# Up-projections of both layers: pairs of tiles by seven block products in place of eight

## The chip, the cores and the metric

The kernel runs on one core of one Trainium2 chip. The time is the device time of one execution in microseconds (us). Everything is float32; dense products use the float32r form of the matmul. Engines: TensorE (PE), VectorE (DVE), ScalarE (ACT), GpSimd (POOL), and SyncE (SP), which only issues DMA transfers.

## The reference, cut to what matters

Two blocks of a transformer-like model over 512 tokens plus 16 meta tokens, width 1024. The first block has two layers, and in each the part that changes is the feed-forward network:

```python
def _sq_relu_mlp(h, w1, w2):
    return jnp.square(jax.nn.relu(h @ w1)) @ w2     # w1: 1024 x 4096, w2: 4096 x 1024

for layer in range(2):
    mix = even_mixer(h, ...) if layer == 0 else retention(h, ...)
    h = layer_norm(ALPHA * h + mix, ...)
    h = layer_norm(ALPHA * h + _sq_relu_mlp(h, w1[layer], w2[layer]), ...)
```

In layer 0 all 528 columns (tokens) are computed (`wide`), in layer 1 only the 512 that the output needs.

## The kernel before, in words

Activations lie feature by feature on the 128 partitions: `x32[:, k, :]` is the k-th of 8 groups of 128 features, over T = 528 tokens. To keep float32 precision each operand is split into a high and a low part (`x_hi`, `x_lo`; `w_hi`, `w_lo`), and each product is three matmuls: w_hi x a_hi, w_hi x a_lo, w_lo x a_hi.

All weights of all stages come as one long stream of chunks, 512 KB each (8 blocks of 128 x 128). SP loads chunk g into slot g mod 4 of `raw` (L217); ACT makes `w_hi` (`split_hi`, L227), DVE makes `w_lo` (`split_lo`, L235), three chunks ahead of PE (`AHEAD`). A slot of `raw` is free when its `w_lo` is made, a slot of `w_hi` and `w_lo` when PE has finished the chunk (`chunk_done`). One chunk is one output tile of 128 features (8 input groups x 3 matmuls, and twice that many of 264 columns where the stage is wide). Four `landed` semaphores count the loads, one for each slot.

The order of each engine's work is written out by hand: each engine has its own program, in which a stage calls a split at the start of each chunk and then what belongs to the finished tile, and each runs strictly in this order. `Mlp` is the feed-forward network. The 4096 hidden features are made in two halves, a and b, of 16 tiles each: stage up (16 chunks), then stage down (16 chunks, which add into x32). For a hidden tile ACT takes the relu out of PSUM (`h_pos`), DVE squares it (`h_sq`), ACT makes `h_hi`, DVE makes `h_lo`. Tiles of a dense stage alternate between PSUM banks 0-1 and 2-3; `evicted` says when a tile is out.

Before `Mlp` stands a layer norm (`ln00`, `ln10`), behind it another (`ln01`, `ln11`). POOL adds squares for the norms, loads constants and, in the attention of layer 0, loads one row of decays for each head (`key_cum`, L492, two buffers). Before that it writes `cum_rows` to DRAM.

Of the kernel before, what the change touches and what calls it, by code (L numbers as in the profile page):

```python
# [7 lines left out]
ALU = mybir.AluOpType  # L8
ACT = mybir.ActivationFunctionType
F32 = mybir.dt.float32  # L10
# [31 lines left out]
STAGES += [("up0a", 16), ("down0a", 16), ("up0b", 16), ("down0b", 16)]  # L42
STAGES += [("ret0", 12), ("ret1", 12), ("ret2", 12), ("ret_out0", 8), ("ret3", 12), ("ret_out1", 8)]
STAGES += [("up1a", 16), ("down1a", 16), ("up1b", 16), ("down1b", 16)]
# [7 lines left out]
FIRST_CHUNK, FIRST_TILE = {}, {}  # L52
_c = _t = 0
for _n, _k in STAGES:
    FIRST_CHUNK[_n], FIRST_TILE[_n] = _c, _t
    _c += _k
    _t += 2 * _k if _n.startswith(("so", "eo")) else _k // KGROUPS.get(_n, 1)
TOTAL_CHUNKS, TOTAL_TILES = _c, _t
# [94 lines left out]
def program(nc, x_in, weights, params, tables, lam_in, w_uk, w_uv, rel, line, skewed, cum_dram, acum_dram, merged_dram, kept_dram, gate_dram, out):  # L153
    with ExitStack() as ctx:
# [55 lines left out]
        def stream_weights(sp):  # L210
            def body(g):
                s = g.mod(RING)
                if not g.stride and g.start == 1:
                    sp.wait_ge(x_landed[3], 16)
                wait(sp, lo_ready, g.at(plus=1 - RING))
                src = weights[one(g), :, :].rearrange("g p n -> p (g n)")
                sp.dma_start(raw[:, s, :, :].rearrange("p k n -> p (k n)"), src).then_inc(landed[s], 16)  # L217
            loop(sp, TOTAL_CHUNKS, RING, body, peel=1)

        def split_hi(act, g):  # L220
# [4 lines left out]
            act.wait_ge(landed[s], g.over(RING).at(16, 16))  # L225
# [247 lines left out]
        def even_loads(pool):  # L473
# [10 lines left out]
            nc.gpsimd.memset(small[:, 13:14], RMS_EPS).then_inc(forget_in, 1)  # L484
            pool.wait_ge(forget_ready, 1)
            pool.dma_start(cum_dram, neg_cum).then_inc(cum_out, 16)
            pool.wait_ge(cum_out, 16)
            for h in range(FOX_HEADS):
# [3 lines left out]
                pool.dma_start(key_cum[:, h % 2], src).then_inc(cum_in[h % 2], 16)  # L492

# [467 lines left out]
        mlp_squared, mlp_hi, mlp_lo = (sem(f"mlp_{n}") for n in ("squared", "hi", "lo"))  # L961
# [241 lines left out]
        class Mlp:  # L1203


            def __init__(self, layer, wide):
                self.layer, self.wide = layer, wide
                placed["next"] = shared
                self.h_hi = at(f"h_hi{layer}", [P, 16, T], F32R)
                self.h_lo = at(f"h_lo{layer}", [P, 16, T], F32R)  # L1210
                self.pos = at(f"h_pos{layer}", [P, 2, T])
                self.sq = at(f"h_sq{layer}", [P, 2, T])

            def pe(self, pe, norm, next_norm):
                for half, hn in enumerate("ab"):
                    pe_stage(pe, f"up{self.layer}{hn}", x_hi, x_lo, self.wide, ready=None if half else norm.ready)
                    pe_stage(pe, f"down{self.layer}{hn}", self.h_hi, self.h_lo, self.wide,
                             ready=(mlp_lo, 32 * self.layer + 16 * half), norm=next_norm if half else None)

            def act(self, act, next_norm):  # L1220
                for half, hn in enumerate("ab"):
                    name = f"up{self.layer}{hn}"

                    def keep(tile, done):
                        u = tile.plus(FIRST_TILE[name])
                        act.wait_ge(chunk_done, done)
                        wait(act, mlp_squared, tile.at(plus=32 * self.layer + 16 * half - 1))
                        nc.scalar.activation(halves(self.pos[:, tile.mod(2)], self.wide), tile_out(u, self.wide), ACT.Relu) \  # L1228
                            .then_inc(evicted[u.mod(2)], 1)
                        act.wait_ge(mlp_squared, tile.at(plus=32 * self.layer + 16 * half + 1))  # L1230
                        nc.scalar.activation(halves(self.h_hi[:, one(tile)].rearrange("p a n -> p (a n)"), self.wide),
# [1565 lines left out]
```

## Time and profile before

| | |
|---|---|
| median of 3 runs | 2895.05 us (2894.86 to 2896.65) |
| profiled execution: its own time | 2897.41 us |
| profiled execution: span of its instructions | 2895.6 us |
| PE busy | 2736.2 us (94%) |
| DVE, ACT, POOL busy | 51%, 38%, 5% of the span |
| mean granted clock of PE | 0.976 of full speed |
| DMA | 248.98 MB, mean 86 GB/s |

Busy times of different engines overlap; they say how full an engine is, not what the end waits for. The chain of waits says that: it is followed back from the last instruction to what released each step. Layer 0's network begins at about 409 us and ends at about 785 us, layer 1's runs from about 1296 to 1660 us.

### The profile page before, as it was taken

Reading aid. Unit: us, or ns where it says so; the run is one execution under the profiler, and the core shown is the slowest. Engines: PE = TensorE matmul, PEld = TensorE weight load, DVE = VectorE, ACT = ScalarE, POOL = GpSimd, SP = SyncE. Lnnn points to the kernel's source line nnn. Section 1 sums busy time; section 2 is a strip of 40 time slices with the busy share of each in tenths; the row PEclk is TensorE's granted clock in tenths of the full one; section 3 lists DMA queues with packets and bytes.
Section 4 is the critical chain, followed back from the end, with each engine's and each line's share of the span. In section 5 each row is a group of like instructions: output and inputs, shape, how many; then the busy total and the mean of one; then the engine's idle time right before and its main releaser. Section 6 shows DMA issues by size and latency. Waiting matters only on the chain.

```text
span 2895.6 us, 39470 instructions
## 1 busy us (share of the span) xinstructions
PE 2736.2 (94%) x14983; PEld 2238.0 (77%) x14983; DVE 1478.1 (51%) x2517; ACT 1095.2 (38%) x1730; POOL 151.2 (5%) x201
## 2 busy tenths in 40 slices
PE   7999989999999999979999989978999998999998
PEld 6877779999987787758888766745777776778786
DVE  3433464233433323264334434865488886664656
ACT  3455443133242322244223344345255454332322
POOL 0000020000100000010000101042000000000000
PEclk9999989999999999989999989999999999999999
DMA  4111112222221121112222224411423332222221
GB/s 154 59 45 45 45 51 94 88 88 94 81 85 63 64 94 63 59 58 95 97 92 96 86 82 117 160 41 56 140 88 117 110 110 102 80 92 97 94 92 68
DMA packets 68107, 248.98 MB, mean 86 GB/s; under 512 B 8056, under 2 KB 8056, under 8 KB 67328
## 3 DMA queue, kind: packets, MB, share of 16 engines
q1 hardware_dynamic: 58256, 210.27, 20.9%
q0 software_dynamic: 7264, 29.36, 3.6%
q10 hardware_dynamic: 2448, 7.41, 0.7%
q8 instruction: 98, 1.61, 0.2%
q14 instruction: 41, 0.34, 0.0%
HBM read 237.44 MB, written 12.71 MB: 86 GB/s over the span
## 4 chain that ended last, share of the span: by engine, by line
PE 82%; DVE 9%; ACT 5%; issue 3%; DMA 1%; POOL 0%; ACTq 0%; DVEq 0%; POOLq 0%
PE ps L264 61%; PE ps L408 6%; PE ps L1339 2%; PE ps L1618 2%; PE ps L756 2%; PE ps L635 2%; PE ps L2140 1%; DVE xs L2282 1%; DVE w_lo L235 1%; PE ps L1327 1%; ACT w_hi L227 1%; PE ps L722 1%; PE ps L1864 1%; DVE seg L2332 1%; DVE ln_xc L1166 1%
## 5 line engine op out<-in xcount | busy, mean ns | idle before, releaser
L264 PE MATMUL ps<-x_hi,w_hi 128*128 128x512 f32 (+1 forms) x2224 | 708.1, 353 | 60.8 <-DVE x_lo L1178 24.2
L235 DVE TENSOR_TENSOR w_lo<-raw,w_hi 128x1024 fp32r<-128x1024 f32 x397 | 492.4, 1241 | 419.1 <-ACT w_hi L227 409.4
L264 PE MATMUL ps<-x_lo,w_hi 128*128 128x512 f32 (+1 forms) x2224 | 703.2, 351 | 0.0
L264 PE MATMUL ps<-x_hi,w_lo 128*128 128x512 f32 (+1 forms) x2224 | 699.8, 349 | 0.0
L227 ACT ACTIVATE w_hi<-raw 128x1024 fp32r<-128x1024 f32 x397 | 416.8, 1052 | 463.3 <-PE ps L264 435.1
L264 PEld LDWEIGHTS ps<-x_hi,w_hi 128*128 128x128 f32 x2224 | 391.3, 190 | 133.2 <-issue 51.4
L264 PEld LDWEIGHTS ps<-x_lo,w_hi 128*128 128x128 f32 x2224 | 390.5, 190 | 56.1 <-issue 1.7
L264 PEld LDWEIGHTS ps<-x_hi,w_lo 128*128 128x128 f32 x2224 | 390.2, 190 | 55.5
L264 PE MATMUL ps<-h_hi,w_hi 128*128 128x264 f32 (+1 forms) x768 | 205.7, 322 | 0.0
L264 PE MATMUL ps<-h_lo,w_hi 128*128 128x264 f32 (+1 forms) x768 | 205.1, 322 | 0.0
L264 PE MATMUL ps<-h_hi,w_lo 128*128 128x264 f32 (+1 forms) x768 | 204.5, 320 | 0.0
L264 PEld LDWEIGHTS ps<-h_lo,w_hi 128*128 128x128 f32 x768 | 127.6, 188 | 11.7 <-issue 0.2
L264 PEld LDWEIGHTS ps<-h_hi,w_lo 128*128 128x128 f32 x768 | 127.8, 189 | 11.2
L264 PEld LDWEIGHTS ps<-h_hi,w_hi 128*128 128x128 f32 x768 | 127.1, 188 | 11.7 <-issue 0.2
L915 DVE SCALAR_TENSOR_TENSOR x<-x,ps 128x512 f32 (+2 forms) x56 | 38.6, 690 | 161.8 <-PE ps L264 161.8
L408 PE MATMUL ps<-x_hi,w_hi 128*128 128x264 f32 x352 | 114.0, 324 | 0.0
L1248 DVE TENSOR_TENSOR h_sq<-h_pos 128x528 f32<-128x528 f32 (+1 forms) x64 | 44.8, 700 | 127.1 <-ACT h_pos L1228 127.1
L408 PE MATMUL ps<-x_hi,w_lo 128*128 128x264 f32 x352 | 103.4, 294 | 0.0
L408 PE MATMUL ps<-x_lo,w_hi 128*128 128x264 f32 x352 | 103.4, 294 | 0.0
L1228 ACT ACTIVATE h_pos<-ps 128x528 f32<-128x528 f32 (+1 forms) x64 | 38.7, 605 | 164.7 <-PE ps L264 164.7
L408 PEld LDWEIGHTS ps<-x_hi,w_hi 128*128 128x128 f32 x352 | 69.7, 198 | 12.2 <-issue 9.9
L688 ACT ACTIVATE s_buf<-s_buf,stat 16x16 f32<-16x16 f32 (+4 forms) x80 | 41.5, 519 | 91.2 <-DVE stat L653 91.2
(392 smaller groups left out, 4055.2 us busy)
## 6 DMA issues: line engine op xcount, KB each, us to landing
raw<-in_weights SPq DMA_DIRECT2D x397, 512.0 KB, 3.2
steps_abc<-acum_rows POOLq DMA_DIRECT2D x16, 512.0 KB, 5.7
bias_skewed<-bias_line POOLq DMA_DIRECT2D x16, 192.0 KB, 7.8
streamed_kept<-kept ACTq DMA_DIRECT2D x12, 256.0 KB, 2.0
x<-in_x_by_feature ACTq DMA_DIRECT2D x4, 528.0 KB, 9.2
key_cum<-cum_rows POOLq DMA_DIRECT2D x8, 264.0 KB, 3.4
bias_near<-bias_skewed POOLq DMA_DIRECT2D x16, 128.0 KB, 2.4
gate_kept<-gate_made ACTq DMA_DIRECT2D x1, 2048.0 KB, 8.3
```

The costliest lines, as they stand in the source:

```text
L227: nc.scalar.activation(w_hi[:, s], raw[:, s], ACT.Copy).then_inc(hi_ready, 1)
L235: nc.vector.tensor_tensor(w_lo[:, s], raw[:, s], w_hi[:, s], ALU.subtract).then_inc(lo_ready, 1)
L264: last = nc.tensor.matmul(o[:, h, :], w[:, s, k], a[:, k0 + k, cols], start=start and k == 0 and n == 0, stop=stop and k == nk - 1 and n == 2)
L408: last = nc.tensor.matmul(ps[:, 2 + h, 0:HALF], a[:, g % RING, w], b[:, k, cols], start=k == 0 and n == 0, stop=half_end and n == 2)
L635: last = nc.tensor.matmul(flat[0:n, o + a:o + b], qk[rows, qt, c:c + n], qk[rows, kt_, a:b], start=True, stop=True)
L688: nc.scalar.activation(s, s, ACT.Exp, scale=-1.0, bias=stat[0:n, 0, u % 64:u % 64 + 1], accum_out=stat[0:n, 1, u % 64:u % 64 + 1]).then_in ...
L756: last = nc.tensor.matmul(flat[rows, o:o + n], vt[0:k, group_of(p) % 2, b, col:col + wide], p_turn[0:k, p % 2, 4 if b == 0 else b - 1, 0:n ...
L915: nc.vector.scalar_tensor_tensor(o, o, factor, tile_out(u, wide), ALU.mult, ALU.add).then_inc(evicted[u.mod(2)], 1)
L1228: nc.scalar.activation(halves(self.pos[:, tile.mod(2)], self.wide), tile_out(u, self.wide), ACT.Relu) \
L1248: nc.vector.tensor_tensor(sq, pos, pos, ALU.mult).then_inc(mlp_squared, 1)
L1339: last = nc.tensor.matmul(flat[:, o + SEQ - w:o + SEQ], rv[0:n, b, e * P:(e + 1) * P], decayed[0:n, b, SEQ - w:SEQ], start=i == 0, stop=i ...
L1618: last = nc.tensor.matmul(kept_out_at(n)[:, 0, :], w[:, ck % RING, k], a[:, k, META:T], start=k == 0 and i == 0, stop=k == KT - 1 and i == 2)
```

## The change

Of the 32 hidden tiles of a layer 28 are now made in pairs, as a product of 2 x 2 blocks: two tiles of output features, by two halves of the input features (groups 0-3 and 4-7), by two halves of the tokens (`cols(0)`, `cols(1)`, 264 each in layer 0, 256 in layer 1). By the form of Strassen and Winograd such a product takes seven products of blocks in place of eight, of sums of blocks of weights and sums of blocks of activations. The first four tiles of half a stay ordinary (`up0a`, `up1a`, 4 chunks). Then `seven0a` makes 6 pairs, `seven0b` 8 pairs, likewise in layer 1.

- A block product (kinds "1" to "7") takes half a chunk: 4 weight blocks x 3 matmuls. A pair takes 7 half chunks, 3.5 chunks, where its two tiles took 2. In all 439 chunks are split in place of 397.
- Weights: kinds 1, 2 and 4 read parts of the old weights; 5, 6, 7 and 3 read sums of weight blocks from a new DRAM tensor `sums_dram`, 4 x 256 KB for each pair. POOL makes these sums with DMA transfers: for each layer eight copies (`sums_copy`), then adding transfers in three steps (`sums_of_two`, `sums_of_three`, `sums_of_four`), each waiting for the one before. For layer 0 the copies are issued at the start, before `cum_rows`, and the steps behind the `key_cum` loads 1, 3 and 5. For layer 1 all stand between `mlp0.pool` and `ln01.pool`. SP waits for a layer's sums before its first seven stage.
- Activations: `pool` makes four sums of blocks from x32; ACT and DVE split them (`turn_hi`, `turn_lo`) during the four ordinary tiles; the fourth overwrites a part of `x_hi` and `x_lo`.
- PSUM: kinds 1, 6, 7 and 4 of a pair accumulate in one bank, with a copy or a sum taken out after each; 5 and 3 in another; 2 in bank 7. ACT copies out after 1, 5 and 6 and takes the relu and square of 4; DVE adds copy and bank after 2, 7 and 3 (into `z`) and squares with the relu. Then ACT makes two `h_hi` (`hidden_pair`, called at the block behind 3), DVE two `h_lo` (`hidden_rest`, called two blocks behind 3).
- Order on PE (`seven_order`), for a pair i in the middle: 1, 2 of i; 7 of i-1; 5, 6 of i; 4, 3 of i-1. The last pair: 1, 2, 7 of i-1, 5, 6, 4 of i-1, 7, 3 of i-1, 4, 3.
- Some semaphores are shared by what had two before (`hidden_hi` for `mlp_hi` and `f_hi_s`, `mixed_hi` for `att_hi_s` and `m_hi_s`), with other counts; every landing adds 32.

```diff
-STAGES += [("up0a", 16), ("down0a", 16), ("up0b", 16), ("down0b", 16)]
+STAGES += [("up0a", 4), ("seven0a", 21), ("down0a", 16), ("seven0b", 28), ("down0b", 16)]
...
+def seven_order(pairs):
+    order = []
+    for i in range(pairs):
+        now = [(kind, i) for kind in "1256"]
+        if i:
+            now = now[:2] + [("7", i - 1)] + now[2:] + [("4", i - 1), ("3", i - 1)]
+        if i == pairs - 1:
+            now = now[:-1] + [("7", i)] + now[-1:] + [("4", i), ("3", i)]
+        order += now
+    return order
...
+        def stream_seven(sp, name):
+            sp.wait_ge(sums_added, SUM_COUNT * (1 + int(name[5])))
+            for b, (kind, i) in enumerate(seven_order(SEVEN[name])):
+                g, half = FIRST_CHUNK[name] + b // 2, b % 2
+                s = g % RING
+                if half == 0:
+                    sp.wait_ge(lo_ready, g + 1 - RING)
+                even = FIRST_SOURCE[name] + 2 * i
+                if kind in "124":
+                    src = weights[even + int(kind == "4"), :, (0 if kind == "1" else 512):(512 if kind == "1" else 1024)]
+                else:
+                    src = sums_dram[FIRST_PAIR[name] + i, :, "5673".index(kind), :]
+                sp.dma_start(raw[:, s, 4 * half:4 * half + 4, :].rearrange("p k n -> p (k n)"), src).then_inc(landed[s], 16)
+        def sums_copy(pool, layer):
+            for name in (f"seven{layer}a", f"seven{layer}b"):
+                for which, row, half in ((0, 1, 0), (1, 0, 0), (2, 1, 0), (3, 0, 1)):
+                    pool.dma_start(sums_at(name, which), quarters(name, row, half)).then_inc(sums_copied, 16)
+        def sums_of_two(pool, layer):
+            pool.wait_ge(sums_copied, SUM_COUNT * (layer + 1))
+            for name in (f"seven{layer}a", f"seven{layer}b"):
+                pool.dma_start(sums_at(name, 0), quarters(name, 1, 1), accum_op=ALU.add).then_inc(sums_added, 16)
+                pool.dma_start(sums_at(name, 2), quarters(name, 0, 0), accum_op=ALU.add).then_inc(sums_added, 16)
+        def sums_of_three(pool, layer):
+            pool.wait_ge(sums_added, SUM_COUNT * layer + 4 * 16)
+            for name in (f"seven{layer}a", f"seven{layer}b"):
+                pool.dma_start(sums_at(name, 1), sums_at(name, 0), accum_op=ALU.add).then_inc(sums_added, 16)
...
+            pool.wait_ge(x_split_lo, KT)
+            sums_copy(pool, 0)
             pool.wait_ge(forget_ready, 1)
             pool.dma_start(cum_dram, neg_cum).then_inc(cum_out, 16)
...
+                if h in (1, 3, 5):
+                    (sums_of_two, sums_of_three, sums_of_four)[h // 2](pool, 0)
...
+            def seven_pe(self, pe, name):
+                summed, kept_ = seven_counts(name, "273"), seven_counts(name, "1564")
+                for b, (kind, i) in enumerate(seven_order(SEVEN[name])):
+                    g = FIRST_CHUNK[name] + b // 2
+                    s = g % RING
+                    if b % 2 == 0:
+                        pe.wait_ge(lo_ready, g + 1)
+                    if kind == "1" and i >= 3:
+                        pe.wait_ge(seven_kept, kept_["4", i - 3])
+                    if kind == "2" and i >= 1:
+                        pe.wait_ge(seven_summed, summed["2", i - 1])
...
+                    if kind in "673":
+                        pe.wait_ge(seven_kept, kept_["165"["673".index(kind)], i])
+                    if kind == "4":
+                        pe.wait_ge(seven_summed, summed["7", i])
+                    if name[6] == "a" and i == 0 and kind in "5674":
+                        pe.wait_ge(turns_lo, 4 * self.layer + "5674".index(kind) + 1)
+                    out_ = self.out_of(kind, i)
+                    for k in range(4):
+                        a_hi, a_lo = self.moving(kind, k)
+                        for n, (w, a) in enumerate(((w_hi, a_hi), (w_hi, a_lo), (w_lo, a_hi))):
+                            last = nc.tensor.matmul(out_, w[:, s, 4 * (b % 2) + k], a, start=kind in "125" and k == n == 0,
                                                    stop=k == 3 and n == 2, skip_group_check=True)
+                    last.then_inc(chunk_done if b % 2 else seven_done, 1)
+                pe.wait_ge(seven_summed, summed["3", SEVEN[name] - 1])
...
+            def seven_act(self, act, name):
...
+                for b, (kind, i) in enumerate(seven_order(SEVEN[name])):
+                    if b % 2 == 0:
+                        split_hi(act, Step(FIRST_CHUNK[name] + b // 2 + AHEAD))
+                    if late is not None:
+                        hidden_pair(late)
+                        late = None
+                    if kind in "156":
+                        self.block_done(act, name, b)
...
+                        nc.scalar.activation(self.copy_of(kind, i), self.out_of(kind, i), ACT.Copy).then_inc(seven_kept, 1)
+                    elif kind == "4":
+                        self.block_done(act, name, b)
+                        r = self.u[:, 2, 0:self.w]
+                        nc.scalar.activation(r, self.out_of("4", i), ACT.Relu, scale=-1.0).then_inc(seven_kept, 1)
+                        act.wait_ge(seven_kept, kept_["4", i])
+                        act_chain.mark(nc.scalar.activation(self.h_raw[:, self.tile_rows(name, i) + 1, self.cols(0)], r, ACT.Square))
+                        act_chain.settle(act)
+                    elif kind == "3":
+                        late = i
+                hidden_pair(late)
+            def seven_dve(self, dve, name):
...
+                for b, (kind, i) in enumerate(order):
+                    if b % 2 == 0:
+                        split_lo(dve, Step(FIRST_CHUNK[name] + b // 2 + AHEAD))
+                    if b in late:
+                        hidden_rest(late.pop(b))
+                    row = self.tile_rows(name, i)
+                    if kind == "2":
+                        self.block_done(dve, name, b)
+                        dve_chain.mark(sum_square(0, i, "1", ALU.max, row, 0))
+                    elif kind == "7":
+                        self.block_done(dve, name, b)
+                        sum_square(1, i, "5", ALU.min, row + 1, 1).then_inc(mlp_squared, 1)
+                    elif kind == "3":
+                        self.block_done(dve, name, b)
+                        sum_square(2, i, "6", ALU.max, row, 1).then_inc(mlp_squared, 1)
+                        late[b + 2] = i
...
             ln00.pool(pool)
+            mlp0.pool(pool, ln00)
+            for part in (sums_copy, sums_of_two, sums_of_three, sums_of_four):
+                part(pool, 1)
             ln01.pool(pool)
```

## Rows read from the trace of the kernel before

**Rows 1.** The profile's page, first part: busy us, share of the span, instructions.

```profile
PE 2736.2 (94%) x14983; PEld 2238.0 (77%) x14983; DVE 1478.1 (51%) x2517; ACT 1095.2 (38%) x1730; POOL 151.2 (5%) x201
```

**Rows 2.** Chain of waits in both layers: start, us, what.

```profile
422.96 328.25 PE ps L264 x2688
...
1379.79 220.38 PE ps L264 x950
```

**Rows 3.** Busy time in one up-projection: length, engines, clock, DMA share, GB/s.

```profile
422.00:504.00 82.00, 81.93 (x670) 81.75 (x669) 39.46 (x45) 32.99 (x45) 0.00 (x0) 1.00 0.26 93
```

**Rows 4.** Splits into w_hi: count, ns min/median/max, first, last start.

```profile
L227 ACT ACTIVATE w_hi<-raw x12: 1042/1044/1047, 431.2 to 495.7; 128x1024 fp32r<-128x1024 f32 x12
...
L227 ACT ACTIVATE w_hi<-raw x14: 1042/1046/1050, 1484.8 to 1557.0; 128x1024 fp32r<-128x1024 f32 x14
```

**Rows 5.** Groups by shape: count, busy us, mean ns, idle before.

```profile
L235 DVE TENSOR_TENSOR w_lo<-raw,w_hi 128x1024 fp32r<-128x1024 f32 x397 | 492.4, 1241 | 419.1 <-ACT w_hi L227 409.4
...
L1251 DVE TENSOR_TENSOR h_lo<-h_sq,h_hi 128x528 f32 x32 | 22.7, 709 | 29.6 <-ACT h_hi L1231 29.6
...
L453 DVE SCALAR_TENSOR_TENSOR x<-x,ps 128x264 f32<-128x264 f32 x16 | 6.8, 426 | 7.8 <-PE ps L408 7.7
...
L227 ACT ACTIVATE w_hi<-raw 128x1024 fp32r<-128x1024 f32 x397 | 416.8, 1052 | 463.3 <-PE ps L264 435.1 <-PE ps L810 10.9 <-PE ps L2140 7.6
...
L1231 ACT ACTIVATE h_hi<-h_sq 128x528 f32 x28 | 18.1, 646 | 24.4 <-DVE h_sq L1248 24.4
...
L461 ACT ACTIVATE qk<-ps 128x264 f32<-128x264 f32 x28 | 10.7, 381 | 21.9 <-PE ps L408 21.9
```

**Rows 6.** Timeline at 423 us: start, us, engine, line, what.

```profile
422.85 0.71 DVE L1248 TENSOR_TENSOR h_sq<-h_pos 128x528 f32<-128x528 f32 x1 [2.93 <-ACT h_pos L1228]
...
423.59 0.65 ACT L1231 ACTIVATE h_hi<-h_sq 128x528 fp32r<-128x528 f32 x1 [0.78 <-DVE h_sq L1248]
...
424.14 1.04 ACT L227 ACTIVATE w_hi<-raw 128x1024 fp32r<-128x1024 f32 x1
```

**Rows 7.** Two gaps of PE (timeline), granted clock behind each (windows).

```profile
364.36 0.51 PE L810 MATMUL ps<-o_hi,w_hi 128*128 128x264 f32 x2 [1.57 <-DVE o_lo L776]
...
366.00:386.00 20.00, 20.00 (x162) 19.52 (x161) 13.64 (x18) 5.32 (x8) 2.80 (x2) 1.00 0.24 79
...
2849.61 0.50 PE L264 MATMUL ps<-f_hi,w_hi 128*128 128x512 f32 x1 [2.19 <-DVE f_lo L2525]
...
2850.00:2858.00 8.00, 8.00 (x30) 6.35 (x29) 4.89 (x7) 2.12 (x2) 0.00 (x0) 0.79 0.18 66
```

**Rows 8.** DMA queues from 1777 to 1796 us; landing there, and usual.

```profile
q0 software_dynamic: 1024, 3.15, 68.7%
q1 hardware_dynamic: 259, 1.00, 15.2%
...
DMA to landing us min/median/max: 3.4/6.8/10.2
...
raw<-in_weights SPq DMA_DIRECT2D x397, 512.0 KB, 3.2
```

**Rows 9.** POOL: an operation by shape (groups), and its timeline.

```profile
L1153 POOL TENSOR_TENSOR ln_xc<-ln_xc,ln_mean 128x528 f32<-128x528 f32 x6 | 10.5, 1778 | 12.5 <-ACT ln_mean L1185 12.5
...
79.88 1.07 POOL L492 DMA_DIRECT2D key_cum<-cum_rows  x2 [1.56 <-DMA cum_rows<-f_row]
193.93 0.54 POOL L492 DMA_DIRECT2D key_cum<-cum_rows  x1 [112.97 <-ACT gate_bias L669]
213.01 0.54 POOL L492 DMA_DIRECT2D key_cum<-cum_rows  x1 [18.55 <-ACT gate_bias L669]
268.65 0.54 POOL L492 DMA_DIRECT2D key_cum<-cum_rows  x1 [22.56 <-ACT gate_bias L669]
290.10 0.54 POOL L492 DMA_DIRECT2D key_cum<-cum_rows  x1 [20.91 <-ACT gate_bias L669]
...
755.03 1.67 POOL L1146 TENSOR_TENSOR ln_sq_sum<-ln_sq 128x528 f32<-128x528 f32 x1 [350.64 <-ACT ln_sq L1134]
```

More of the change, by code:

```diff
@@ L150, with program @@
 TABLES = _c
[L153 removed]
+def program(nc, x_in, weights, params, tables, lam_in, w_uk, w_uv, rel, line, skewed, cum_dram, acum_dram, merged_dram, kept_dram, gate_dram, sums_dram, out):
     with ExitStack() as ctx:
@@ new lines, in program, with quarters, sums_at @@
+        sums_copied, sums_added = sem("sums_copied"), sem("sums_added")
+        SUM_COUNT = 8 * 16
+        def quarters(name, row, half):
+            n = SEVEN[name]
+            blocks = weights[FIRST_SOURCE[name]:FIRST_SOURCE[name] + 2 * n, :, 512 * half:512 * half + 512]
+            return blocks.rearrange("(a two) p n -> two p a n", two=2)[row]
+        def sums_at(name, which):
+            n = SEVEN[name]
+            return sums_dram[FIRST_PAIR[name]:FIRST_PAIR[name] + n, :, which, :].rearrange("a p n -> p a n")
@@ L1220, in act @@
             def act(self, act, next_norm):
-                for half, hn in enumerate("ab"):
[L1222 to L1231, printed above, removed]
-                                             halves(self.sq[:, tile.mod(2)], self.wide), ACT.Copy).then_inc(mlp_hi, 1)
-                    side_stage(act, split_hi, name, keep, peel=int(self.layer == half == 0))
+                name = f"up{self.layer}a"
@@ new lines, in act @@
+                for t in range(4):
+                    u = Step(FIRST_TILE[name] + t)
+                    split_hi(act, Step(FIRST_CHUNK[name] + t + AHEAD))
+                    if t == 2:
+                        self.turn_hi(act, 0)
+                        self.turn_hi(act, 1)
+                    elif t == 3:
+                        self.turn_hi(act, 2)
+                    act.wait_ge(chunk_done, FIRST_CHUNK[name] + t + 1)
+                    wait(act, mlp_squared, 32 * self.layer + t - 1)
+                    nc.scalar.activation(halves(self.pos[:, t % 2], self.wide), tile_out(u, self.wide), ACT.Relu).then_inc(evicted[u.mod(2)], 1)
+                    act.wait_ge(mlp_squared, 32 * self.layer + t + 1)
+                    nc.scalar.activation(halves(self.h_hi[:, t], self.wide), halves(self.sq[:, t % 2], self.wide), ACT.Copy).then_inc(hidden_hi, 1)
@@ L2476, in ffn_pe @@
                 loop(pe, 8, 4, lambda t: chunk_products(pe, f"fd{g}", t, f_hi, f_lo, False, nk=n,
-                                                        ready=(f_lo_s, done) if not t.stride and t.start == 0 else None), peel=1)
+                                                        ready=(hidden_lo, HIDDEN + done) if not t.stride and t.start == 0 else None), peel=1)
                 done += n
```

243 lines of the change are left out of this document (193 added, 50 removed).

## The prediction

> **What bounds the kernel now.** I read the busy line first: TensorE (PE) works 94% of the span [rows 1]. The chain of waits then shows that nothing else counts where the change is: from 422.96 us, in the first up-projection, the chain stays on the matmuls of L264 for 328 us, and in layer 1 it covers the whole stretch asked for [rows 2]. The busy time by stage says how far the others are from it: in an up-projection PE is busy all 82 us at full clock, VectorE (DVE) 48%, ScalarE (ACT) 40%, the DMA engines 26% [rows 3]. So a matmul saved there is time saved, if the other two engines can follow a stage that asks more of them.
>
> The price of a tile comes from the splits `w_hi`, one for each chunk of weights and in step with PE: 11 periods from 431.2 to 495.7 us are 5.864 us a tile in layer 0 (48 matmuls of 264 columns, 0.1222 us each), 13 periods from 1484.8 to 1557.0 us are 5.554 us in layer 1 (24 of 512 columns, 0.2314 us each) [rows 4].
>
> **Matmuls removed.** In each layer 28 of the 32 tiles become 14 pairs. A pair takes 7 blocks x 4 x 3 = 84 matmuls of half the tokens, where two tiles took 96 such halves. Layer 0: 28 x 5.864 = 164.2 us before; 14 x 84 x 0.1222 = 143.7 after: 20.5 us less. Layer 1 changes its shape too: 512 columns become 256, which no float32r row shows. The line through the two prices gives 0.44 ns a column and 0.1187 us at 256. 28 x 5.554 = 155.5 us before, 14 x 84 x 0.1187 = 139.6 after: 15.9 us less. If 256 columns cost as much as 264 (a fixed price of the weight load), it is 11.8. I take the line, since 264 to 512 columns lie on a slope near the column rate. Together -36.4 us. The prices hold one boundary per 48 or 24 matmuls; now there is one per 12, with one to three waits. I add 3 us for 140 more boundaries at 0.02 us (between 0 and 8: a hand-over of [rows 6] is up to 0.04 us, with two semaphores 0.06 by estimate).
>
> **Work added to ACT and DVE.** Each pair brings 3.5 chunks to split instead of 2, at 1.05 us on ACT (`w_hi`) and 1.24 on DVE (`w_lo`) [rows 5]. ACT further has three copies of half a bank (0.38 each), a relu, a square (0.38 each), two `h_hi` (0.65). DVE has three sums and three squares of 264 (0.43 each) and two `h_lo` (0.71). That is 6.8 us on ACT and 8.2 on DVE, within the 10.26 us of a pair: by throughput both fit. Both run strictly in program order, though, so I followed the order by hand. Rows show that a hand-over between the engines costs 0.03 to 0.04 us and that neighbours on one engine overlap by up to 0.1 [rows 6].
>
> A block takes T = 1.466 us. The tight wait is that of block 4 of pair i-1: it accumulates into the bank that DVE must have read for block 7. Where a pair's block 1 begins a chunk (odd i), the slice ends with: block 4 done at 6T; ACT relu and square 0.76; `w_hi` 1.05; DVE `w_lo` 1.23, in front of the sum of block 3; sum and square 0.86; ACT two `h_hi` 1.29, copy of block 1 0.38, `w_hi` 1.05; DVE `w_lo` 1.23, two `h_lo` 1.42, sum and square of block 2 0.86, sum of block 7 0.43. That is 10.6 us of instructions, 10.3 with overlaps and hand-overs. PE wants its next block 4 six blocks later, after 6T = 8.8 us: it stands 1.5 us. In the next pair the splits fall elsewhere (no `w_lo` between blocks 3 and 2, one less in the chain) and the same reckoning leaves 1.2 us to spare. So one stall per two pairs: two in the part of six pairs, three in that of eight, 5 x 1.5 = 7.5 us in layer 0. In layer 1 T is 1.424, the instructions some 0.15 us shorter in all, the stall 1.6: 8 us.
>
> The last pair brings its blocks closer together: block 4 comes two blocks after its block 7, whose sum stands behind a `w_lo` (0.65 us late), and PE may not start down before the sum of block 3, behind a `w_lo` and two `h_lo` (1.25 us late). 1.9 x 4 stages = 7.6 us. At the first pair the fourth turned operand and its splits push the copy of block 1 by 0.2 to 0.5 us, twice. Stalls together 24 us (bounds: 16 with each chain 0.5 us shorter, 32 with each 0.5 longer).
>
> **The turned operands.** Four POOL operations over 4 x 264 columns: twice the 1.78 us of one of 528 [rows 9] is 3.6 us each, 14 us from the last `norm_y` at about 417 us. The first is needed by block 5 at about 437 us, the last by block 4, later; four ordinary tiles (until 434 us) cover them. Without that cover they would cost up to 14 us. The counts that replace `mlp_hi` and others move nothing.
>
> **The sums in DRAM.** A layer copies 14 pairs x 4 x 256 KB = 14.7 MB and adds as much in three steps that wait for each other. The nearest row is the copy from DRAM to DRAM at 1777 us: 3.15 MB in 19 us beside a little of `raw`, 166 GB/s, and a `raw` load issued into it took 10.2 us in place of 3.2 [rows 8]. The copies take 89 us at that rate. No row shows an adding transfer: at least that rate's 89 us, and 177 if each byte counts twice. I take 100.
>
> Layer 0 has from 20 us to about 400: copies until 109 us; the adds sit between `key_cum` loads of POOL, the steps issued at about 109, 213 and 269 us, each with 30 to 80 us before the next load [rows 9]. What is queued behind them is `cum_rows`, the first two `key_cum` loads, which serve the heads after the first third of the stage, and later the next loads, double-buffered by one spacing (21 us or more). Cost nothing; if the adds take double, the last step lasts from 269 to 313 us and the load of 290 is late by some 5 us.
>
> Layer 1's start at about 432 us, beside seven0a: copies until 521, adds until 620, the next work of POOL is at 755 us [rows 9]. Seven0a wants a chunk every (10.26 + 0.75) / 3.5 = 3.15 us instead of 5.86. A slot of `raw` is turned round in landing + `w_hi` + `w_lo`, and there are four: (3.2 + 2.3) / 4 = 1.4 us undisturbed, (10.2 + 2.3) / 4 = 3.1 beside copies. It just fits; I take 3 us for late splits in that stage and the start of seven0b (0 to 30: a landing of 14 us gives 4.1 us a chunk, 0.95 x 21 = 20 us, and 10 more in seven0b if the adds reach it).
>
> The Trainium skill, "DMA: Bandwidth & Descriptors", section "Queues, rings and completion order", says that each DMA engine serves its queues in turn, a packet from each. The row agrees that `raw` suffers beside the POOL queue (10.2 us). By the rule alone, with this profile's packets of 0.18 us for `raw` and 0.20 for the other queue (16 engines x 19 us x 15.2% / 259, and x 68.7% / 1024), a chunk of 8 packets an engine takes 3.1 us, and the sum above would stand without its 3 us. The same page, section "Rules for kernel authors", says that an accumulating transfer reads its destination before it writes it; no row here shows one. It speaks for the doubled price.
>
> **Sum.** -36.4 + 3 + 24 + 3 = -6.4 us. The profiled execution took 2897.4 us (span 2895.6), so it would be 2891.0; that execution is 2.4 us above the median of 2895.05, so I forecast 2888.6. Its own range is 2880 to 2896.
>
> **Rivals.**
> A. The side engines hide: if the chain of block 4 is under 8.8 us and the ends cost half, only some 4 us of the 24 remain: -26, 2869. For it: ACT 67% and DVE 80% busy by throughput. Against: the order above, whose durations are all rows. Half of the stalls gone gives 2877.
> B. The clock falls with the stalls (the other side). A PE gap of 1.57 us left the granted clock at 1.00; after one of 2.19 us it was 0.79 over 8 us, that is 3.4 us at 1.2 instead of 2.4 GHz, worth 1.7 us [rows 7]. If the stall is 2.0 instead of 1.5 us, each of the 10 costs 0.5 + 1.7 and some ends 1.7 too: +22 to +26, 2913. It decides from a stall of about 2 us.
> C. The copies starve `raw` in seven0a (landing 14 us or more): +20 to +30, 2909 to 2919. For it: a stage that wants almost twice the rate beside 29 MB of foreign traffic. Against: four slots and three split chunks ahead.
> D. Adding is several times dearer than copying: key loads of layer 0 and the sums for `ln01` at 755 us come late: +20 and more, 2910 to 2950.
> E. Small losses eat the rest: 256 columns at 0.1222 us (+4), boundaries at their bound (+5): 2894 to 2898, no change.
> That the change does not remove the matmuls is excluded; the counts are fixed.
>
> **Chances.** Forecast 0.37, A 0.20, B 0.15, C 0.12, D 0.05, E 0.11. 0.2% is 5.8 us, about what a measurement here tells from no change. Faster (under 2889.3): half of the forecast and all of A, 0.39. Same (to 2900.8): most of the other half, E and mild C, 0.27. Slower: B, D, most of C, 0.34. The range reaches from A's half to B and C: 2868 to 2920.
>
> **What would show it.** Matmul groups of 264 and 256 columns at 84 a pair; seven0a about 66 us, seven0b about 88. PE waits for a DVE sum into `z` in pairs 2, 4 and 6 of a stage, 1 to 2 us each, and before down. `raw` landing 6 to 11 us between 432 and 620 us with few ACT waits on it. Granted clock 1.00 within the stages. I am wrong if PE waits for `w_lo` (C), if the clock is below 0.97 there (B), or if POOL is still adding after 700 us (D).

## The result and the profile after

Before: 2894.58 us median of 10 runs (2888.54 to 2904.15); after: 2916.49 us, also of 10 (2906.35 to 2921.48). The ratio is 1.0071, 95% interval 1.0054 to 1.0087. The change made the kernel about 20 us slower. I had forecast 2888.6, 6 us faster. The range that I gave, 2868 to 2920 us, holds the result; the direction was wrong.

The profiled execution took 2910.66 us. Its page, with the lines that answer to [rows 1]:

```profile
span 2908.9 us, 40169 instructions
PE 2708.8 (93%) x15319; PEld 2235.9 (77%) x15319; DVE 1573.0 (54%) x2679; ACT 1158.1 (40%) x1864; POOL 211.0 (7%) x241
...
PE 75%; DVE 10%; ACT 7%; issue 4%; DMA 3%; POOL 0%; ACTq 0%; DVEq 0%; SPq 0%; POOLq 0%
```

PE is 27 us less busy than before and the span is longer: the matmuls were saved, and the time went into gaps and into matmuls at a lower clock. The last line is the chain of waits by engine, and 3% of it is DMA.

To place the loss I took the first matmul of each up-projection and of the stage behind the network, in both traces. Layer 0's network took 391.1 us before (408.81 to 799.88) and 405.3 after (403.57 to 808.90), layer 1's 387.9 (1295.89 to 1683.76) and 392.7 (1305.92 to 1698.63): +14.3 and +4.8. Outside the networks the run after is 5.2 us shorter ahead of the first, 1.0 longer between the two and 1.6 shorter behind. That is within what runs differ by: r1_after (below) is the same kernel and starts its first network at 408.63 us, as before.

The four changed stages, as windows (length, busy time of PE, PE's weight loads, DVE, ACT, POOL, granted clock, DMA share, GB/s), in the order seven0a, seven0b, seven1a, seven1b:

```profile
430.00:519.00 89.00, 70.18 (x506) 67.94 (x505) 53.62 (x75) 41.87 (x67) 6.17 (x5) 0.90 0.99 316
612.00:701.00 89.00, 83.50 (x680) 82.55 (x678) 61.06 (x89) 50.59 (x82) 0.00 (x0) 1.00 0.51 161
1331.00:1403.00 72.00, 62.60 (x505) 61.46 (x504) 52.19 (x74) 42.18 (x69) 0.00 (x0) 0.95 0.52 161
1493.00:1580.00 87.00, 80.73 (x674) 79.78 (x672) 60.81 (x90) 50.02 (x82) 0.00 (x0) 1.00 0.54 166
```

From the first matmul to the last they take 88.0, 87.9, 71.8 and 86.0 us. The two b stages are what the prediction's prices give (eight pairs of 10.26 us, three stalls and an end: 88.5; in layer 1 86.5). The two a stages are not: my terms give 69.8 for seven0a (six pairs, two stalls, an end, a start and 3 us for `raw`; the "about 66 us" at the prediction's end leaves out the last two) and 65.3 for seven1a. They are 18 and 6.5 us over, and that is nearly the whole difference between forecast and result. In the first line the DMA engines are busy 99% and the clock is 0.90. Two things fill seven0a's 88 us beside its 504 matmuls, which at full clock are 61.6: PE stands still for 18 us, and the matmuls take the remaining 8 us more, at the lower clock. In seven1a these are 9.4 and 2.6 us.

What is waited for between 403 and 520 us (us in total, times, longest):

```profile
DVE w_lo L323 <- ACT w_hi L315: 31.9, 17, 3.7
ACT w_hi L315 <- DMA raw<-weight_sums: 20.9, 9, 4.5
...
PE ps L1407 <- DVE h_z L1473: 9.0, 5, 4.1
...
PE ps L1407 <- ACT h_u L1449: 7.4, 3, 3.5
...
ACT w_hi L315 <- DMA raw<-in_weights: 7.1, 4, 2.9
```

PE's matmuls are never seen waiting for a weight, and its weight loads only for 2.1 us in two waits (`PEld ps L1407 <- DVE w_lo L323`). PE waits for copies and sums, which stand in program order behind a split on ACT or DVE, and the split waits for `raw`: 28 us in 13 waits. The chain of the same stretch names the transfers and how long they took:

```profile
441.80 10.94 DMA raw<-weight_sums
...
455.47 16.03 DMA raw<-in_weights
...
474.24 14.48 DMA raw<-weight_sums
```

These answer to [rows 8]: 10.9, 16.0 and 14.5 us, where I had used 10.2. Each is a load of 256 KB, half a chunk in rows of 2 KB; that row was one of 512 KB in rows of 4 KB. Meanwhile POOL (timeline; in brackets what it waited for):

```profile
411.87 2.46 POOL L1332 TENSOR_TENSOR t_raw<-x 128x1056 f32<-128x1056 f32 x1 [12.72 <-ACT x L1289]
414.41 2.81 POOL L1334 TENSOR_TENSOR t_raw<-t_raw,x 128x1056 f32<-128x1056 f32 x1
417.30 3.33 POOL L1336 TENSOR_TENSOR h_raw<-t_raw,x 128x1056 f32<-128x1056 f32 x1
420.60 2.95 POOL L1337 TENSOR_TENSOR t_raw<-x 128x1056 f32<-128x1056 f32 x1
423.47 6.75 POOL L290 DMA_DIRECT2D weight_sums<-in_weights  x8
488.62 1.44 POOL L295 DMA_DIRECT2D weight_sums<-in_weights  x1 [58.40 <-DMA weight_sums<-in_weights]
...
548.93 2.93 POOL L301 DMA_DIRECT2D weight_sums<-weight_sums  x2 [54.35 <-DMA weight_sums<-in_weights]
578.77 2.93 POOL L306 DMA_DIRECT2D weight_sums<-weight_sums  x2 [26.91 <-DMA weight_sums<-weight_sums]
```

The copies of layer 1's sums run from 423 to 489 us, inside seven0a. The adds go on for over 90 us in down0a, where one of the normal chunks lasts over 5.8 us, and hurt nobody: PE is busy 93.86 of the 94 us between seven0a and seven0b. And DVE, beside POOL's four operations:

```profile
411.10 0.71 DVE L1272 TENSOR_TENSOR x_lo<-x,x_hi 128x528 fp32r<-128x528 f32 x1 [0.69 <-ACT x_hi L1295]
412.50 2.40 DVE L1272 TENSOR_TENSOR x_lo<-x,x_hi 128x528 fp32r<-128x528 f32 x1 [0.70 <-ACT x_hi L1295]
414.82 3.48 DVE L323 TENSOR_TENSOR w_lo<-raw,w_hi 128x1024 fp32r<-128x1024 f32 x1
418.23 2.97 DVE L1545 TENSOR_TENSOR h_sq<-h_pos 128x528 f32<-128x528 f32 x1
421.91 2.20 DVE L1547 TENSOR_TENSOR h_lo<-h_sq,h_hi 128x528 fp32r<-128x528 f32 x1 [0.71 <-ACT h_hi L1526]
```

The same operations take 0.71, 1.24, 0.71 and 0.71 us elsewhere [rows 5, 6]. Four of them take 11.05 us together in place of 3.4.

So two theories to test. **D**: the transfers for layer 1's sums starve `raw` in seven0a. **P**: POOL's four operations hold DVE up at the start of each network. A third cost, **S**, was forecast: the order of ACT and DVE makes PE stand once in two pairs. It shows in seven0b, where the chain starts anew on the matmuls every 22.15 us (two pairs are 20.5):

```profile
636.44 0.35 DVE h_z L1473
637.17 0.43 DVE h_z L1473
637.74 11.90 PE ps L1407 x96
...
659.89 11.92 PE ps L1407 x96
```

### The profile page after: what moved, and what is told of

The parts are those of the page before. It is cut to its first block, busy times and chain, and to the rows that moved or that the text cites. A ratio compares the mean times of both kernels' runs of the same rounds, so it can differ in the third digit from the quotient of the medians.

```text
span 2908.9 us, 40169 instructions
## 1 busy us (share of the span) xinstructions
PE 2708.8 (93%) x15319; PEld 2235.9 (77%) x15319; DVE 1573.0 (54%) x2679; ACT 1158.1 (40%) x1864; POOL 211.0 (7%) x241
## 4 chain that ended last, share of the span: by engine, by line
PE 75%; DVE 10%; ACT 7%; issue 4%; DMA 3%; POOL 0%; ACTq 0%; DVEq 0%; SPq 0%; POOLq 0%
PE ps L352 50%; PE ps L496 5%; PE ps L1407 5%; PE ps L1916 2%; PE ps L1637 2%; ACT w_hi L315 2%; PE ps L848 2%; PE ps L727 2%; DVE w_lo L323 1%; PE ps L2438 1%; DMA raw<-in_weights 1%; DMA raw<-weight_sums 1%; PE ps L1625 1%; PE ps L814 1%; ACT x L1289 1%
## 5 line engine op out<-in xcount | busy, mean ns | idle before, releaser
L323 DVE TENSOR_TENSOR w_lo<-raw,w_hi 128x1024 fp32r<-128x1024 f32 x439 | 548.8, 1251 | 513.5 <-ACT w_hi L315 509.8
L352 PE MATMUL ps<-x_hi,w_hi 128*128 128x512 f32 (+1 forms) x1552 | 530.2, 368 | 61.3 <-DVE x_lo L1272 25.1
L352 PE MATMUL ps<-x_lo,w_hi 128*128 128x512 f32 (+1 forms) x1552 | 524.0, 364 | 0.0
L352 PE MATMUL ps<-x_hi,w_lo 128*128 128x512 f32 (+1 forms) x1552 | 520.9, 362 | 0.0
L352 PEld LDWEIGHTS ps<-x_hi,w_hi 128*128 128x128 f32 x1552 | 280.0, 191 | 124.1 <-issue 52.6
L352 PEld LDWEIGHTS ps<-x_lo,w_hi 128*128 128x128 f32 x1552 | 279.4, 191 | 46.5 <-issue 1.7
L352 PEld LDWEIGHTS ps<-x_hi,w_lo 128*128 128x128 f32 x1552 | 279.3, 191 | 46.0
L1407 PE MATMUL ps<-x_hi,w_hi 128*128 128x264 f32 (+1 forms) x448 | 130.2, 291 | 24.3 <-DVE h_z L1473 24.3
L1407 PE MATMUL ps<-x_hi,w_lo 128*128 128x264 f32 (+1 forms) x448 | 128.6, 287 | 0.0
L1407 PE MATMUL ps<-x_lo,w_hi 128*128 128x264 f32 (+1 forms) x448 | 128.6, 287 | 0.0
L1407 PE MATMUL ps<-t_hi,w_hi 128*128 128x264 f32 (+1 forms) x336 | 97.0, 289 | 14.5 <-ACT h_u L1449 10.1
L1407 PEld LDWEIGHTS ps<-x_hi,w_hi 128*128 128x128 f32 x448 | 86.8, 194 | 27.4 <-issue 17.9
```

The costliest lines, as they stand in the source:

```text
L323: nc.vector.tensor_tensor(w_lo[:, s], raw[:, s], w_hi[:, s], ALU.subtract).then_inc(lo_ready, 1)
L352: last = nc.tensor.matmul(o[:, h, :], w[:, s, k], a[:, k0 + k, cols], start=start and k == 0 and n == 0, stop=stop and k == nk - 1 and n == 2)
L1407: last = nc.tensor.matmul(out_, w[:, s, 4 * (b % 2) + k], a, start=kind in "125" and k == n == 0, stop=k == 3 and n == 2, skip_group_check ...
```

## The experiments

Nine kernels, in three groups, each group on one chip with the kernel before beside it. Times are medians; the ratio, to the kernel before on that chip, has its 95% interval. An alteration is put to the changed kernel.

**r1_after**: unaltered.

> The changed kernel unaltered, as the common base of this group. Theory D (the transfers that make layer 1's sums starve the weight loads of seven0a), theory S (the program order of ACT and DVE alone makes the loss) and theory P (POOL's four operations on the turned operands slow DVE down at the start of each layer) all expect the recorded ratio again, 1.005 to 1.009 to the kernel before.

Measured: 2909.41 us, before 2891.89; ratio 1.0063 (1.0043 to 1.0082). Stages 88.8, 88.0, 71.6 and 86.0 us. Stage times repeat within 1 us, so from here on a stage tells more than the total.

**r2_late_sums**: layer 1's sums are made later.

```diff
 # ret_loads, once for each head h
+                (sums_copy, sums_of_two, sums_of_three, sums_of_four)[h](pool, 1)
 # POOL's program, behind mlp0.pool
-            for part in (sums_copy, sums_of_two, sums_of_three, sums_of_four):
-                part(pool, 1)
```

> Layer 1's copies and adds are issued behind the decay loads of the retention instead of beside seven0a and down0a. Theory D: ACT's waits on raw in seven0a vanish, the stage shrinks from 89 to about 70 us, 14 to 22 us less than the changed kernel (ratio to before about 1.000). Theory S: under 5 us less, since the order of the engines stays. The transfers now lie beside ret0, which asks for half the rate, and should cost nothing there.

Measured: 2899.23, ratio 1.0021 (1.0009 to 1.0034). Seven0a 73.0 us in place of 88.8, the other three unchanged (87.9, 71.7, 85.9). The window of seven0a (columns as above) and the waits in it:

```profile
434.00:508.00 74.00, 64.72 (x510) 63.57 (x508) 53.12 (x74) 43.02 (x69) 0.00 (x0) 0.98 0.52 157
...
ACT w_hi L315 <- PE ps L1407: 4.6, 6, 1.2
PE ps L1407 <- DVE h_z L1473: 3.8, 3, 1.5
```

No wait for `raw` is left; the splits wait for PE, as they should. D is shown, and it is worth 15.8 us in the stage, 12 by the ratio. The total fell short of the 14 to 22 us expected, and the stage of its "about 70". Of the 15.8 us 9.8 are idle time of PE (18.9 to 9.1 us) and 6 are clock (0.87 over the stage in r1_after, 0.98 here): the gaps cost more than their length. The transfers cost nothing where they now lie: from the end of the first network to the start of the second it is 499.5 us, 499.3 in r1_after.

**r3_order**: the block's own work (copies on ACT, sums and squares on DVE) ahead of the splits; DVE's `split_lo` and `hidden_rest` move as `split_hi` does here.

```diff
 # seven_act and seven_dve, for each block b
-                    if b % 2 == 0:
-                        split_hi(act, Step(FIRST_CHUNK[name] + b // 2 + AHEAD))
...
+                    if b % 2 == 0:
+                        split_hi(act, Step(FIRST_CHUNK[name] + b // 2 + AHEAD))
 # h_lo of a pair
-                        late[b + 2] = i
+                        late[b + 3] = i
```

> In the seven stages ACT and DVE make their splits behind the work of the block instead of ahead of it, and DVE makes h_lo three blocks after block 3 instead of two. Sums, copies and products are the same. By the chain worked out in the prediction the stall of 1.5 us per two pairs and most of the two waits at the end go: 14 to 20 us less than the changed kernel, a little less if seven0a stays starved of weights (theory D). Theory S expects 20 us or more less, and that seven0a shrinks with it. Rival: the stall is only a place where another wait shows, and under 5 us go.

Measured: 2915.99, ratio 1.0081 (1.0065 to 1.0098): not better, a miss. The stages did get shorter (86.7, 83.0, 67.7, 81.1), so the stall of two pairs is gone. But from the end of seven0a to the start of seven0b it is 100.7 us where r1_after has 94.6, and behind the other stages 4 to 5 us more as well. The timeline of DVE at the end of seven0b:

```profile
707.45 1.22 DVE L323 TENSOR_TENSOR w_lo<-raw,w_hi 128x1024 fp32r<-128x1024 f32 x1 [3.06 <-ACT w_hi L315]
708.59 0.42 DVE L1473 TENSOR_TENSOR h_z<-h_u,ps 128x264 f32<-128x264 f32 x1
```

The last sum now stands behind a `w_lo` whose `w_hi` comes late, and PE waits for that sum 3.8 us (0.7 in r1_after) before the down-projection. The granted clock is 0.87 from 705 to 710 us and 0.79 from 710 to 715. What was won in the middle was lost at the end.

**r7_middle**: as r3_order, but the last ten blocks of a stage in the old order.

```diff
+LAST_BLOCKS = 10
...
+                middle = len(order) - LAST_BLOCKS
 # new order while b < middle, the changed kernel's order from there on
...
-                        late[b + 2] = i
+                        late[b + 2 + (b + 3 < middle)] = i
```

> The order of run r3_order (block work ahead of the splits on ACT and DVE, h_lo one block later), but in the last ten blocks of each stage the order of the changed kernel again. Theory S with its end: r3_order gained the 1.5 us per two pairs and gave them back only at the end of each stage, where the last sum stood behind a w_lo and h_lo tiles. Then the wait of PE at the end is 0.7 us again instead of 3.8, the time from one of the four stages to the next stands as in the unaltered kernel (94.6 and 90.4 us behind the a stages), seven0b takes 82 to 84 us, seven1b 80 to 82, and the kernel is 12 to 18 us faster than the unaltered one (2893 to 2898 us). Rival G, the order makes later splits and so costs in the down-projections too: the time behind the stages stays 4 to 6 us longer, and nothing is gained in all.

Measured: 2905.14, before 2893.83; ratio 1.0039 (1.0024 to 1.0054). Stages 88.4, 83.8, 68.4, 81.9, and behind seven0a 94.9 us again. The waits of PE from 616 to 702 us:

```profile
PE ps L1410 <- DVE h_z L1479: 0.9, 3, 0.5
PE ps L355 <- DVE h_z L1479: 0.7, 1, 0.7
```

0.9 us in three waits in place of 5.4 in four. S and its end are confirmed; G falls. The gain in all is 7 us by the ratios, less than the 12 to 18 expected, and the intervals overlap; the stages carry the finding. Three of them gain 3 to 4 us each. Seven0a gains nothing: there the splits wait for `raw` whatever their order. (In r8_all_middle, where they don't, it gains 5.)

**r4_turns_dve**: the four operations for the turned operands on DVE, two in each of the first two tiles (the first of the four is shown).

```diff
-                nc.gpsimd.tensor_tensor(t1, x32[:, 0:4, first], x32[:, 0:4, second], ALU.subtract)
+                nc.vector.tensor_tensor(t1, x32[:, 0:4, first], x32[:, 0:4, second], ALU.subtract)
...
```

> The four operations that make the turned operands run on DVE (1.25 us each, two behind the split of tile 0, two behind that of tile 1) instead of on POOL. Theory P: DVE's operations at the start of a layer take their usual 0.7 to 1.25 us instead of 2.2 to 3.5, PE no longer waits for t_lo and for the copy of block 1, 8 to 11 us less than the changed kernel (4 to 6 in each layer). Rival: the program order of ACT and DVE in the four ordinary tiles makes these waits, and under 3 us go.

Measured: 2906.95, ratio 1.0053 (1.0033 to 1.0073). Seven1a 68.5 in place of 71.6 and seven0a 84.6. On DVE the operations take 1.22 us each and its neighbours their usual time (the timeline, layer 1):

```profile
1308.73 1.23 DVE L323 TENSOR_TENSOR w_lo<-raw,w_hi 128x1024 fp32r<-128x1024 f32 x1 [0.25 <-ACT w_hi L315]
1309.88 1.22 DVE L1333 TENSOR_TENSOR t_raw<-x 128x1024 f32<-128x1024 f32 x1
```

P is shown, at 3 us in layer 1. Only 1.1 us of these are idle time of PE (9.0 to 7.9 us); the rest is clock. In the changed kernel two gaps of PE follow each other at the start of seven1a, and the granted clock is 0.76 over the ten microseconds from 1340 (timeline, and a window as above):

```profile
1336.60 0.36 PE L1407 MATMUL ps<-t_hi,w_hi 128*128 128x256 f32 x1 [2.56 <-DVE t_lo L1354]
...
1341.07 0.58 PE L1407 MATMUL ps<-t_hi,w_hi 128*128 128x256 f32 x1 [2.71 <-ACT h_u L1449]
...
1340.00:1350.00 10.00, 8.93 (x61) 8.94 (x62) 8.50 (x11) 5.01 (x8) 0.00 (x0) 0.76 0.48 154
```

In r4_turns_dve the first of the two is shorter, and the clock stays at 1.00 over the whole stage:

```profile
1327.79 0.36 PE L1409 MATMUL ps<-t_hi,w_hi 128*128 128x256 f32 x1 [0.97 <-DVE t_lo L1356]
...
1332.26 0.39 PE L1409 MATMUL ps<-t_hi,w_hi 128*128 128x256 f32 x1 [2.81 <-ACT h_u L1451]
```

In the total P is not told from nothing (the intervals of 1.0063 and 1.0053 overlap), and it is less than the 8 to 11 us expected: PE still waits 2.8 us for the copy of block 1. POOL does nothing then, so that wait is one of program order. ACT stands idle for 2.7 us until DVE has squared the fourth tile (the square comes behind a `w_lo` and two `t_lo`), and then makes `h_hi`, `turn_hi` and a `w_hi` before the copy.

**r9_late_turns**: r2_late_sums and r4_turns_dve together. **r8_all_middle**: those two and r7_middle.

> Two alterations at once: the second layer's sums are made in the retention stage (as in r2_late_sums), and the turned operands are made on DVE (as in r4_turns_dve). If their gains stand side by side (10 to 12 us and 2.5 to 4 us or more by the medians): 2884 to 2892 us here, a ratio of 0.997 to 1.000 to the kernel before, with the first of the four stages at 69 to 70 us. If the gain of the turned operands was only that of a stage that waited for raw anyway, no more than the first alteration: 2897 to 2899 us.

> All three alterations at once: late sums for the second layer, turned operands on DVE, and the new order of ACT and DVE in all but the last ten blocks of a stage. If the three costs named (raw starved by the copies, POOL beside DVE at the start, the splits ahead of the block work) are separate and are all that kept the change from its gain: stages of 65, 83, 64 and 81 us and 2868 to 2880 us, a ratio of 0.992 to 0.996, faster than the kernel before. If another cost takes their place (the clock, or the next engine in turn): 2884 us or more.

Measured: r9_late_turns 2891.30, ratio 0.9995 (0.9979 to 1.0012), stages 71.4, 87.9, 68.5, 85.9. r8_all_middle 2879.52, ratio 0.9948 (0.9929 to 0.9967), stages 66.3, 83.8, 65.3, 81.9. The gains add up, and with all three the idea is faster than the kernel before, by 0.5%. Both totals lie in the ranges expected, seven0a somewhat above (71.4 for 69 to 70, 66.3 for 65). In layer 0 the operations on DVE are worth 1.6 us of the stage (73.0 to 71.4), where I had expected 4 to 6. The windows of the four stages of r8_all_middle:

```profile
431.00:498.00 67.00, 63.37 (x507) 61.76 (x505) 52.02 (x73) 41.73 (x67) 0.00 (x0) 1.00 0.54 170
592.00:676.00 84.00, 83.02 (x674) 81.95 (x673) 60.15 (x89) 50.62 (x82) 0.00 (x0) 1.00 0.56 170
1307.00:1373.00 66.00, 61.78 (x507) 60.15 (x505) 51.38 (x74) 41.65 (x67) 0.00 (x0) 1.00 0.58 174
1463.00:1545.00 82.00, 80.56 (x673) 79.56 (x671) 59.36 (x89) 50.00 (x82) 0.00 (x0) 1.00 0.58 174
```

PE is busy 288.7 of 299 us, with a granted clock of 1.00 in all four. The new order is worth 16 us in the four stages here (0.9995 to 0.9948: 14), now that none of them starves.

**r6_whole_rows** and **r10_short_rows** ask why `raw` suffers. The changed kernel loads a chunk of these stages in two transfers with rows of 2 KB, where it was one with rows of 4 KB. Both kernels multiply other weight blocks than they should and serve for their times alone.

```diff
 # stream_seven, r6_whole_rows: once for each chunk
+                    whole_src = weights[FIRST_SOURCE[name] + b // 4, :, :]
+                    sp.dma_start(raw[:, s, :, :].rearrange("p k n -> p (k n)"), whole_src).then_inc(landed[s], 32)
+                continue
 # r10_short_rows: for each block, halves of rows, never from the sums
+                src = weights[even + int(kind in "4567"), :, (0 if kind in "157" else 512):(512 if kind in "157" else 1024)]
```

> The changed kernel, but the weights of the four shortened stages are loaded as whole chunks in rows of 4 KB, one transfer a chunk, in place of two transfers of 2 KB rows; the sums in DRAM are made as before (the products then read other blocks than they should, the bytes loaded are the same, and so is the work of every engine). Theory W, the short rows of 2 KB lose their share of the DMA engines to the copies' larger packets and only therefore raw comes late: the first of the four stages falls from 88 us to 75 to 79 us, and the kernel by 9 to 13 us. Rival V, copies and loads together simply ask for more than the DMA engines carry, whatever the packets: the stage stays at 84 to 89 us and the kernel within 4 us of the unaltered one.

> The control to run r6_whole_rows: again every weight block of the four stages is read from the weights and none from the sums, but as in the changed kernel in two transfers of 256 KB a chunk with rows of 2 KB (the products read other blocks than they should; bytes and work of the engines are the same, and the sums are still made). Theory W, the row length decides: the first stage takes 86 to 89 us and the kernel is as slow as the unaltered one, 1.005 to 1.008 of the kernel before. Rival, what helped in r6_whole_rows was that nothing was read from the sums' tensor while the copies wrote to it: the stage takes 74 to 79 us here too, and the ratio is about 1.003.

Measured: r6_whole_rows 2904.31, ratio 1.0027 (1.0013 to 1.0042), seven0a 75.4 us. r10_short_rows 2907.81, before 2891.35, ratio 1.0061 (1.0041 to 1.0081), seven0a 86.4 us. The queues over 45 us in the middle of the copies (packets, MB, share of 16 engines), r6_whole_rows from 445 us:

```profile
q0 software_dynamic: 2791, 11.04, 65.1%
q1 hardware_dynamic: 1801, 6.56, 36.6%
```

and r10_short_rows from 432 us:

```profile
q0 software_dynamic: 2898, 11.46, 68.9%
q1 hardware_dynamic: 2798, 5.10, 32.4%
```

The queue of the copies is served alike in both. With short rows `raw` gets as many packets as the copies do (2798 to 2898), and only 5.1 MB in 45 us, 113 GB/s. With whole rows it gets fewer packets but 6.6 MB, 146 GB/s; that is nearly all it asks for, since without the copies (r2_late_sums, 45 us from 440) it takes 7.1 MB. Theory W is shown, and V falls: the form of the loads decides 11 of the 16 us. Row length and the number of transfers changed together, so these two are not told apart. That it is read from the sums' tensor explains at most the 2.4 us between 88.8 and 86.4.

## Why the prediction was wrong

**The matmuls: right.** -36.4 us. Two pairs take 22.15 us in seven0b: 20.5 and a stall, as priced. A matmul of 256 columns, which no row had, comes out on the line: in seven1b the median from the start of one to the next is 0.118 us, where I had 0.1187. The 3 us for more boundaries were not needed: from block to block it is 1.456 us in seven0b where PE does not wait, and T was 1.466.

**The stalls: right.** 1.5 us every second pair (5.4 us of PE's waits in seven0b, with an end of 0.8, and 0.7 more before down: the ends are 1.5 us, not 1.9). Rival A falls with it. In the sum of DVE's work I slipped: the parts give 8.3 us a pair, not 8.2, which changes nothing.

**The clock: the sign of rival B came true, for another reason.** As I put it B needed longer stalls in the steady part; there the clock stayed at 1.00 in both b stages. But it was 0.90 over seven0a and 0.95 over seven1a, and the slower matmuls make 8 and 2.6 us of these stages. My sum has no clock in it for gaps that come of C or at the start. Nor does it decide from one stall of about 2 us: in r4_turns_dve a gap of 2.81 us behind one of 0.97 left the clock at 1.00, while gaps of 2.56 and 2.71 in the changed kernel left 0.76 over ten microseconds. So one such gap did not lower it; what decides is not shown.

**"It just fits; I take 3 us": wrong, the main error.** It was 16 (r1_after against r2_late_sums), 10 as idle time of PE and 6 by the clock. Two inputs of that sum failed. I took the landing from a row in which `raw` came in rows of 4 KB, once in a while; the change asks for a chunk every 3.15 us in rows of 2 KB. And the copies were faster than I thought, 14.7 MB in 65 us (226 GB/s, not 166), so heavier neighbours. By the landings that the chain shows, (14 + 2.3) / 4 gives 4.1 us a chunk, 20 us in 21 chunks; this is the bound that I had written down and set aside. A forecast that balances at 3.1 against 3.15 has no margin, and should have been put near the middle of its range. Rival C named this mechanism, and its 2909 to 2919 holds the result. That is in part luck: it counted only on `raw`, of its 20 to 30 us 16 came, and the start of the stages made up for the rest.

The Trainium skill, "DMA: Bandwidth & Descriptors", section "Queues, rings and completion order", says that an engine takes packets from its queues in turn. The nearly equal counts of r10_short_rows agree, if a turn holds as many of the profile's packets for one queue as for the other; r6_whole_rows can't test it, since `raw` gets nearly what it asks for. In the prediction I followed that rule with the long packets of before: halving the packet halves what a turn is worth.

**"Four ordinary tiles cover them": wrong.** They covered the operations, not what these did to DVE. Four DVE operations took 7.6 us longer, then PE waited for `t_lo` (1.8 us in layer 0, 2.6 in layer 1) and for the copy of block 1 (2.7 in layer 1). Of the 6.5 us by which seven1a exceeds my terms, moving the operations to DVE gives back 3.1, most of it by the clock; the rest is near the 2.8 us that PE still waits there for block 1's copy. I had priced the whole start at 0.2 to 0.5 us. I had searched for what waits for POOL, and not for who works beside it.

The DVE rows show how it is held up: `x_lo` begins at 412.50 and ends at 414.90, when POOL's first operation had ended at 414.33; the next three end 1.1, 0.6 and 0.6 us after one of POOL's. The Trainium skill, "SBUF — State Buffer", section "Who interferes with whom", says that a DVE instruction with two SBUF inputs contends with a GpSimd instruction that reads SBUF, and that the ports they share are an exclusive lock. This trace agrees (2.40 us in place of 0.71). The prediction did not ask for it.

**Sums in DRAM: the time right by two errors.** Copies 65 us, not 89. Adds dearer, not 100 in all: the first step, 7.3 MB, lasts from 488.62 to 548.93, 122 GB/s, the second, 3.7 MB, 29.8 us, 123 GB/s. So an added byte costs 1.85 times a copied one (the loads beside them were not the same), all 14.7 MB some 120 us. Rival D's late loads did not come. In layer 0 the step before a key load was issued at 262.85, the next load 21.5 us after the last, as in [rows 9], and the sums for `ln01` at 764 us, 182 us after the last add was issued:

```profile
262.29 0.57 POOL L582 DMA_DIRECT2D key_cum<-cum_rows  x1 [19.84 <-ACT gate_bias L761]
262.85 3.05 POOL L306 DMA_DIRECT2D weight_sums<-weight_sums  x2
283.75 0.60 POOL L582 DMA_DIRECT2D key_cum<-cum_rows  x1 [17.85 <-ACT gate_bias L761]
...
764.06 1.67 POOL L1240 TENSOR_TENSOR ln_sq_sum<-ln_sq 128x528 f32<-128x528 f32 x1 [182.35 <-ACT ln_sq L1228]
```

**The sum.** My terms were -4.4 us for layer 0 and -2.2 for layer 1. The networks measured +14.3 and +4.8: 25.7 us more in all. Seven0a has 18.2 of it: 13 by transfers above the 3 allowed, the rest at its start, where PE still waits 2.4 us for `t_lo` and 2.9 for the copy of block 1 in r2_late_sums. Seven1a has 6.5, and the b stages are 1.1 us under my terms. Outside the four stages the networks take 5.0 us more than before; 3.0 of these are PE's waits of 0.7 to 0.8 us before down, which my terms held inside the stages as ends, and 2 are not accounted for. The 3 us for boundaries go off.

**Still open.** What the wait for block 1's copy (1.9 us even in r8_all_middle) would be without `turn_hi` ahead of it, or with DVE's square of the fourth tile ahead of the `t_lo`, was not tried, nor were sums stored as whole chunks, so that a load has rows of 4 KB beside copies.

## What to carry to other kernels

Where a change makes a stage ask for data faster, look at everything that the DMA engines do in that stage, and in what packets: with rows of 2 KB the weight loads got 113 GB/s beside the copies, with rows of 4 KB 146. Bulk transfers that nothing waits for belong into a stage with slack, and moving them there was a change of three lines and gave 12 us. Work that is moved to an idle engine must be checked against those that work at the same time, not only against those that wait for it. And an order that removes a stall in the steady part of a loop is to be checked at its last turn. Gaps of TensorE are to be priced with the granted clock behind them: here it added 6 us to 10.

## What the runs showed of the hardware

- A transfer from DRAM to DRAM that adds moves 122 GB/s of result beside one load stream, a copying one 226 GB/s.
- Beside a stream of copies on POOL's queue, loads in rows of 2 KB got 113 GB/s, in rows of 4 KB 146 GB/s (nearly all the stage asked for), with the copies at 245 to 255 GB/s either way.
- A POOL operation over SBUF holds up a DVE operation with two inputs from SBUF, which then ends 0.6 to 1.1 us after the POOL operation: 0.71 us became 2.2 to 3.0, 1.24 became 3.5.
- A matmul of 256 columns in float32r follows the one before after 0.118 us; the line through 264 and 512 columns gives 0.1187.
- A gap of PE of 2.81 us behind one of 0.97 left the granted clock at 1.00; gaps of 2.56 and 2.71 us with one block of matmuls between them left 0.76 from 1340 to 1350 us.
